# Second attention of a fused two-block layer: the order of scores, transposes and values inside odd steps, and the PSUM banks of its opening

## What is computed

```
s = jnp.einsum('bqhd,bkhd->bhqk', q, k) * scale      # causal, or masked by the top-k selection
p = masked_softmax(s, mask)
o = jnp.einsum('bhqk,bkhd->bqhd', p, v)
o_nsa = g0 * o_cmp + g1 * o_slc + g2 * o_win
o = jnp.concatenate([o_nsa, o_dsa], axis=-1) @ w_out[l]
```

## Time and profile before

| what | value |
|---|---|
| median of 3 runs | 1789.47 us (1789.26 to 1789.98) |
| the profiled execution, its time | 1787.86 us |
| its span, first to last instruction | 1786.1 us |
| PE busy | 1763.6 us (99%) |
| DVE / ACT / POOL busy | 974.3 (55%) / 382.4 (21%) / 1181.0 us (66%) |
| mean granted TensorE clock | 0.997 |
| PE, scores (L1378) in the chain that ended last | 2% of the span |
| PE, transposes (L1389) in it | 2% |
| PE, values (L1409) in it | 2% |

### The profile page before, as it was taken

One profiled execution on the slowest core, in us unless ns is written; L12 is line 12 of the kernel. 1 busy time (PEld: TensorE's weight loads), 2 busy tenths in 40 slices (PEclk: granted clock), 3 DMA queues, 4 the chain that ended last, 5 costly groups with the idle time before them and its releaser, 6 DMA issues.

```text
span 1786.1 us, 24918 instructions
## 1 busy us (share of the span) xinstructions
PE 1763.6 (99%) x8821; PEld 1394.4 (78%) x8821; DVE 974.3 (55%) x1664; ACT 382.4 (21%) x827; POOL 1181.0 (66%) x1182
## 2 busy tenths in 40 slices
PE   8999999999999999999999999999999999999998
PEld 6888888887876788888888888878446778888887
DVE  4855345544655105565514556799874887007613
ACT  3111000012246211211100001455884110000001
POOL 4676767675665477677677768755754677668862
PEclk9999999999999999999999999999999999999999
DMA  9655465542330132455435543513000322333221
GB/s 355 215 189 176 141 206 186 161 153 66 100 99 25 36 107 94 142 171 188 125 110 191 188 127 94 127 50 95 25 25 1 95 71 96 114 96 93 95 94 48
DMA packets 245549, 212.93 MB, mean 119 GB/s; under 512 B 45986, under 2 KB 240991, under 8 KB 245471
## 3 DMA queue, kind: packets, MB, share of 16 engines
q1 hardware_dynamic: 229440, 211.18, 37.0%
q10 hardware_dynamic: 16030, 0.72, 0.5%
HBM read 209.72 MB, written 2.10 MB: 119 GB/s over the span
## 4 chain that ended last, share of the span: by engine, by line
PE 70%; POOL 13%; issue 9%; DVE 5%; DMA 1%; ACT 1%; ACTq 0%; POOLq 0%; DVEq 0%
PE ps L768 19%; PE ps L770 18%; PE ps L769 18%; POOL w_lo L697 8%; POOL w_hi L692 2%; PE ps L1378 2%; POOL w_hi L691 2%; PE ps L1389 2%; PE ps L1149 2%; PE ps L1409 2%; DMA raw<-in_ffn_w_down 1%; PE ps L1170 1%; PE ps L1158 1%; PE ps L809 1%; DVE tt L2260 0%
## 5 line engine op out<-in xcount | busy, mean ns | idle before, releaser
L697 POOL TENSOR_TENSOR w_lo<-raw,w_hi 128x512 fp32r<-128x512 f32 (+4 forms) x576 | 736.3, 1307 | 11.8
L768 PE MATMUL ps<-h_hi,w_hi 128*128 128x512 f32 x1192 | 467.8, 392 | 1.8 <-DVE h_lo L2552 1.4
L770 PE MATMUL ps<-h_hi,w_lo 128*128 128x512 f32 x1192 | 464.8, 390 | 0.0
L769 PE MATMUL ps<-h_lo,w_hi 128*128 128x512 f32 x1192 | 464.6, 390 | 0.0
L689 POOL TENSOR_TENSOR w_hi<-raw,ones 128x8 fp32r<-128x8 f32 x144 | 33.3, 232 | 449.5 <-PE ps L770 385.3
L768 PEld LDWEIGHTS ps<-h_hi,w_hi 128*128 128x128 f32 x1192 | 223.9, 188 | 54.4 <-issue 5.9
L770 PEld LDWEIGHTS ps<-h_hi,w_lo 128*128 128x128 f32 x1192 | 223.9, 188 | 47.3
L769 PEld LDWEIGHTS ps<-h_lo,w_hi 128*128 128x128 f32 x1192 | 224.0, 188 | 46.2
L768 PE MATMUL ps<-g_hi,w_hi 128*128 128x512 f32 x608 | 237.7, 391 | 0.1
L770 PE MATMUL ps<-g_hi,w_lo 128*128 128x512 f32 x608 | 236.6, 389 | 0.0
L769 PE MATMUL ps<-g_lo,w_hi 128*128 128x512 f32 x608 | 236.6, 389 | 0.0
(11 more groups left out here) (408 smaller groups left out, 2405.6 us busy)
## 6 DMA issues: line engine op xcount, KB each, us to landing
ada<-in_ada_w SPq DMA_DIRECT2D x31, 1024.0 KB, 7.0
ada<-in_w_ada SPq DMA_DIRECT2D x24, 1024.0 KB, 7.2
raw<-in_ffn_w_gate SPq DMA_DIRECT2D x22, 1024.0 KB, 5.3
raw<-in_ffn_w_up SPq DMA_DIRECT2D x22, 1024.0 KB, 5.2
raw<-in_w_in SPq DMA_DIRECT2D x16, 1024.0 KB, 5.1
raw<-in_w_up SPq DMA_DIRECT2D x16, 1024.0 KB, 5.3
raw<-in_w_down SPq DMA_DIRECT2D x16, 1024.0 KB, 4.8
raw<-in_ffn_w_down SPq DMA_DIRECT2D x16, 768.0 KB, 4.8
```

Source lines behind the costliest of these rows:

```text
L697: last = pool.tensor_tensor(lo[:, c], src[:, c], hi[:, c].bitcast(F32), ALU.subtract)
L768: pe.matmul(o, wh, xh, start=start, stop=False)
L769: pe.matmul(o, wh, xl, start=False, stop=False)
L770: return pe.matmul(o, wl, xh, start=False, stop=stop)
```

## The change

On PE, the steps with an even number keep the order scores, transposes, values. Those with an odd number have the reverse: values, transposes, scores. So the values of an even step are followed by the values of the next, and the scores of an odd step by those of the next. Which step is worked, how far the lags reach, and every wait in front of a step's scores, transposes and values stay as they are, except in the opening. ACT, DVE and POOL keep their order in the steps.

In the opening the banks are exchanged. The fourth bank of the scores is 7 in place of 0. The outputs use 6 and 0 in place of 6 and 7. The compressed transposes go to the banks 6 and 3 in place of 4 and 6, and wait for rotation 12 on DVE (`rp_out`), which reads bank 3. The scores of step 1 now wait for the copy of the compressed values out of bank 7 (`cm_kv_ev`, DVE line 2520) in place of ACT's copies of the compressed probabilities; the second tile of the transposes waits for those. ACT does the exps of step 0 ahead of the two compressed copies.

```diff
--- before.py
+++ after.py
@@ -654,7 +654,7 @@
     MLA_STEPS = 2 * MLA_HEADS
     LAG_T1, LAG_V1 = 2, 3
     B_S, B_T, B_O = (0, 1, 2, 4), (3, 5), (6, 7)
-    B_S2, B_T2 = (1, 5, 4, 0), (2, 3)
+    B_S2, B_T2, B_O2, B_CT = (1, 5, 4, 7), (2, 3), (6, 0), (6, 3)
     def turned1(t):
 
         return (sq, tt)[t // 2 % 2][:, t % 2]
@@ -1381,8 +1381,10 @@
         def pair_transposes(s):
             for t in (2 * s, 2 * s + 1):
                 pe.wait_ge(pr_p, t + 1)
-                if t < 2:
+                if t == 0:
                     pe.wait_ge(rp_out, ROT1 + 14)
+                elif t == 1:
+                    pe.wait_ge(cm_ev, 2)
                 else:
                     pe.wait_ge(at_ev, PAIR_T0 + t - 1)
                 for c in range(s % 4 + 1):
@@ -1391,7 +1393,7 @@
 
         def compressed_values(c):
             for g in range(NSA_KV):
-                pe.matmul(ps[HD * g:HD * g + HD, B_O[c % 2]], v_diag[:, g, c, :], ptc[:, g, :], start=True, stop=False)
+                pe.matmul(ps[HD * g:HD * g + HD, B_O2[c % 2]], v_diag[:, g, c, :], ptc[:, g, :], start=True, stop=False)
 
         def pair_values(pi, j):
 
@@ -1406,7 +1408,7 @@
                     if pi < 8:
                         compressed_values(c)
             for side, x in enumerate(PAIRS[pi]):
-                last = pe.matmul(ps[HD * side:HD * side + HD, B_O[c % 2], P * j:T], x["v"](j),
+                last = pe.matmul(ps[HD * side:HD * side + HD, B_O2[c % 2], P * j:T], x["v"](j),
                                  turned(8 * pi + side)(PT_ROW * j + P * j, T - P * j),
                                  start=pi >= 8 and j == 0, stop=chunk_ends(pi) and j == 3)
             if j == 3:
@@ -1414,30 +1416,44 @@
 
         def turn_compressed():
             pe.wait_ge(cm_sub, 2)
+            pe.wait_ge(rp_out, ROT1 + 13)
             for b in range(2):
                 pe.wait_ge(cm_p, b + 1)
                 for gr in range(2):
                     for q in range(2):
-                        last = pe.transpose(ps[:, 4 + 2 * b, P * (2 * gr + q):P * (2 * gr + q) + P],
+                        last = pe.transpose(ps[:, B_CT[b], P * (2 * gr + q):P * (2 * gr + q) + P],
                                             cs[:, b, P * (2 * q + gr):P * (2 * q + gr) + P], ident)
                 last.then_inc(cm_tr, 1)
+
+        def scores_step(s):
+            if s < PAIR_STEPS:
+                pair_scores(s)
+
+        def transposes_step(s):
+            if LAG_T <= s < PAIR_STEPS + LAG_T:
+                pair_transposes(s - LAG_T)
+
+        def values_step(s):
+            pi, j = values_at(s)
+            if pi is not None:
+                pair_values(pi, j)
 
         pe.wait_ge(rp_rot, ROT1 + 13)
         pe.wait_ge(cm_hid_ev, 2)
         for s in range(PAIR_STEPS + LAG_V + 1):
             if s == 1:
                 turn_compressed()
-                pe.wait_ge(cm_ev, 2)
-                pe.wait_ge(rp_rot, ROT1 + 14)
+                pe.wait_ge(cm_kv_ev, 2)
             if s == 32:
                 pe.wait_ge(kd_up, 1)
-            if s < PAIR_STEPS:
-                pair_scores(s)
-            if LAG_T <= s < PAIR_STEPS + LAG_T:
-                pair_transposes(s - LAG_T)
-            pi, j = values_at(s)
-            if pi is not None:
-                pair_values(pi, j)
+            if s % 2 == 0:
+                scores_step(s)
+                transposes_step(s)
+                values_step(s)
+            else:
+                values_step(s)
+                transposes_step(s)
+                scores_step(s)
 
         pe.wait_ge(o_lo_done, 12)
         for i in range(8):
@@ -1877,10 +1893,12 @@
             act.activation(cs[:, b], cs[:, b], ACT.Exp, scale=HD ** -0.5).then_inc(cm_exp, 1)
         raw_copy(12)
         raw_copy(13)
-        for b in range(2):
+
+        def compressed_turned(b):
             act.wait_ge(cm_tr, b + 1)
             act.copy(ptc[:, :, 2 * P * b:2 * P * b + 2 * P],
-                     ps[:, 4 + 2 * b].rearrange("p (g q) -> p g q", g=2)).then_inc(cm_ev, 1)
+                     ps[:, B_CT[b]].rearrange("p (g q) -> p g q", g=2)).then_inc(cm_ev, 1)
+
         def pair_turn(t):
             qc, pi = t // 2 % 4, t // 8
             act.wait_ge(at_tr, PAIR_T0 + t + 1)
@@ -1899,13 +1917,16 @@
             c = finished_at(s)
             if c is not None:
                 act.wait_ge(pr_pv, (s - LAG_V) // 4)
-                act.copy(h_hi[:, c], ps[:, B_O[c % 2]]).then_inc(o_hi_done, 1)
+                act.copy(h_hi[:, c], ps[:, B_O2[c % 2]]).then_inc(o_hi_done, 1)
             for t in (2 * (s - LAG_T), 2 * (s - LAG_T) + 1):
                 if 0 <= t < 2 * PAIR_STEPS:
                     pair_turn(t)
             for t in (2 * s, 2 * s + 1):
                 if t < 2 * PAIR_STEPS:
                     pair_exp(t)
+            if s == 0:
+                for b in range(2):
+                    compressed_turned(b)
 
         root_table(act)
         norm_squares(act, 4, y_ready, 0, y2)
@@ -2549,7 +2570,7 @@
             c = finished_at(s)
             if c is not None:
                 dve.wait_ge(o_hi_done, PAIR_C0 + c + 1)
-                dve.tensor_tensor(h_lo[:, c], ps[:, B_O[c % 2]], h_hi[:, c].bitcast(F32), ALU.subtract).then_inc(o_lo_done, 1)
+                dve.tensor_tensor(h_lo[:, c], ps[:, B_O2[c % 2]], h_hi[:, c].bitcast(F32), ALU.subtract).then_inc(o_lo_done, 1)
             if 4 <= s < 32 and s % 4 < 3:
                 select(1)
```

## The result

The change makes the kernel slower: 1799.56 us in the median (1797.48 to 1802.16, 6 runs) against 1789.56 us before (1787.98 to 1789.98, 6 runs), 10.0 us more. The ratio is 1.0055, with a 95% interval of 1.0044 to 1.0065.

What follows compares the result with a forecast made beforehand. The prediction took PE to be full in the second attention, with ACT's copies closing a chain once the odd steps are reversed. Costs of 6.7 + 1.8 less 0.7 made 7.8 us slower: 1797.3 us, range 1793.0 to 1801.0.

Steps and rivals of the forecast that it cites:

- Part 1, what PE saves: PE's groups of one kind behind each other save 0.15 or 0.20 us each, 7.9 us gross; four steps in 7.80.
- One sign that the prediction named: PE's waits before the scores of the middle of the second attention should be gone; no size given.
- Part 2, the ring: Odd steps of the second attention: a closed chain over ACT and PE, 9.25 us per four steps against 8.50; cost 6.7.
- The legs: Three links per four steps: scores 4k + 3 to transposes 4k + 2, to the next pair's values, to scores 4k + 7.
- the second leg: From the transposes of step 4k + 2 to the values of the next pair, over ACT's copies: 4.08 us.
- Part 3, the opening: Start up to the scores of step 7: 2.2 us won, spent again with 0.8 more, 1.0 for half clock; cost 1.8.
- Part 4, the end: From the scores of step 47 to the output projection: 10.5 us against 11.16, a gain of 0.7.
- The sum: Whole kernel: 6.7 + 1.8 - 0.7 = 7.8 us slower, forecast 1797.3 us.
- The saved changes: Rival: PE's saving comes through in the second attention, period 7.80 us, time 1781.6 us; chance 0.08.
- The clock: Rival: PE's new waits halve its clock in a third of the stretches, 12 us on top, 1809 us; chance 0.07.

Runs made afterwards that it cites:

- the other parity: The changed kernel with the even steps reversed and the odd ones in the order scores, transposes, values: 1787.73 us against 1790.42 before, ratio 0.9987.
- the cut scaling: The changed kernel with POOL scaling only 128 of the 384 columns in the steps 4k + 2: 1797.01 us in one run.

## Why the prediction was right, and where it was off

**Part 1, what PE saves: right.** The period without waits was to be 7.80 us; the other parity shows 7.79. The 0.20 us for scores behind scores, which was chosen between two bounds, was measured at 0.2 (1.28 us for 512 and 128 columns, 1.70 for 384 and 512). The rule of the Trainium skill cited there ("TensorEngine Tiling (Array Packing)", Key Properties) agrees with these rows: groups of the same mode behind each other save the fixed part, groups of another mode pay it. One sign that the prediction named was empty: waits before the scores of the middle could not go, since before there were none.

**Part 2, the ring: right in its place and its size, with one term missing.** The legs were forecast at 3.80, 4.08 and 1.37 us and measured at 3.81, 4.08 and 1.37. The extra copy on ACT, which passes in full into the periods of the new order and not at all into those of the old, shows that the ring is closed over ACT; the cut scaling shows that POOL's scaling doesn't set it. For the second leg the evidence is weaker: the trace names ACT's copies before the values of 512 columns in every period, and the wait is gone in the middle where the steps 4k + 3 keep the old order, but no run stretched this leg by itself. What failed is the sentence that DVE is not in the way and that the chain is the same up to step 31. There the period is 9.46 us, 0.19 more. In DVE's view, the maxima of step 19, whose scores start at 1297.79:

```profile
1299.05 0.69 DVE L2550 CUSTOM_DVE_ANT_0 p<-ps,kst 128x512 f32<-128x512 f32 x1 [0.43 <-DVE score L2430]
```

and behind step 31 those of step 35:

```profile
1338.32 0.69 DVE L2550 CUSTOM_DVE_ANT_0 p<-ps,score 128x512 f32<-128x512 f32 x1 [3.23 <-PE ps L1378]
```

The maxima start 1.26 us after the scores (1297.79 to 1299.05), against 1.16 behind step 31 (1337.16 to 1338.32). DVE had ended its selection round before, so it isn't the round's length. Each of the two legs that go over the maxima loses 0.1 us, and without the rounds the period is 9.26. So six of the ten periods between step 7 and step 47 were 0.2 longer than forecast and the others 0.02, 1.3 us in all: 96.41 us (1268.55 to 1364.96) where 95.1 were forecast. The cost of part 2 is 96.41 - 88.44 = 8.0 us, where 6.7 was said.

**Part 3, the opening: 2.5 us where 1.8 was said.** The steps of it came as forecast: the reciprocal 3.82 us after the first scores (forecast 1252.0 - 1248.13 = 3.9), the transposes 6.19 (6.2). From step 3 on the legs at full clock would have put the scores of step 7 at 16.7 us; they came at 18.39, with 6.8 us at half clock. That leaves 1.7 us for the clock, where I had taken 1.0. The excess goes with the half clock: 1.6 of it lie in the second leg, from the transposes at 1260.64 to the compressed values at 1266.31, or 5.67 us where 4.08 was forecast; in the run with the short scaling the same leg (1259.33 to 1263.50) ran at full clock and took 4.17. The prediction also read only one stretch of half clock in the opening of before, where there are two.

**Part 4, the end:** a gain of 0.6 us, where 0.7 was said.

**The sum:** 8.0 + 2.5 - 0.6 = 9.9 us in the stage, where 7.8 was forecast; the time lies in the range (1793.0 to 1801.0), though the middle and the opening both cost more than was said.

**The rivals.** The saved changes did not come through, though only because of the parity: turned the other way, up to 0.7 us of each period do. The clock stayed at 1.00 in the periods, with PE busy for 17.2 to 17.6 of 20 us; that rival did not come.

## What to carry to other kernels

A full engine tells what is saved by taking work from it only as long as the others' results still arrive in time; before an order is turned, follow each producer's own order once around and add up the links, taken from a place of the trace where the full engine has run out of other work (here the end of the stage). Turn the order in those steps whose results are short and whose copies stay covered: the same edit cost 8 us in one parity and gained up to 0.7 us a period in the other. And read with care which engine a wait is put down to when two arrive close together; here lengthening ACT's side by 0.5 us and shortening POOL's by 0.2 us a tile settled it.

## What the runs showed that was not expected

DVE starts its maxima 0.1 us later after the scores when its last instruction before was one of a selection round, although the round had ended 0.4 us earlier; without the rounds the 0.1 us are gone (1295.04 to 1296.20, 1.16 us). What makes them is open; no run here separated the parts of that wait.

In the opening the granted clock was 0.50 (the 1.2 GHz level) for 3.4 us in some executions and for 6.8 in others of nearly the same program; the scores of step 7 came after 17.51 us with the first and after 18.39 with the second. Ahead of the stage, where all these kernels are the same, the half clock sorts the executions too: the five profiles with 3.4 us of it start the stage at 1248.0 to 1248.3, the eight with 6.8 us at 1249.6 to 1250.4, and the one with 10.2 us (the other parity) at 1252.3. A single profile can be 2 to 4 us off for that reason alone, which is why the stage is measured from its first scores.
